# Feature pairs of a SwiGLU feed-forward in seven block products instead of eight, in a two-layer encoder step

## The chip, the cores and the metric

The kernel runs on one core of one Trainium2 chip, as one launch. The metric is device time in microseconds. TensorE (PE) multiplies, VectorE (DVE), ScalarE (ACT) and GpSimd (POOL) do everything else, and SyncE (SP) issues all DMAs.

## The reference

One inference step of a two-layer encoder on 512 prompt tokens and 8 x 16 sample tokens, T = 640 columns in all, D = 1024, F = 2816. It has four SwiGLU feed-forwards (two for each layer), a latent attention between the first two and a window attention between the last two:

```python
def swiglu(x, w_gate, w_up, w_down):
    return (jax.nn.silu(x @ w_gate) * (x @ w_up)) @ w_down
...
    for layer in range(DEPTH):
        x = x + FFN_RES * swiglu(rms_norm(x, P['ffn_norm1'][layer]), P['ffn1_w_gate'][layer],
                                 P['ffn1_w_up'][layer], P['ffn1_w_down'][layer])
        h = rms_norm(x, P['mix_norm'][layer])
...
        x = x + y
        x = x + FFN_RES * swiglu(rms_norm(x, P['ffn_norm2'][layer]), P['ffn2_w_gate'][layer],
                                 P['ffn2_w_up'][layer], P['ffn2_w_down'][layer])
```

## The kernel before

**Layout.** The residual stands transposed in SBUF: eight tiles of 128 of the 1024 model dimensions (`x`), each with 640 token columns, worked on in two halves h of 320 columns. A matrix product in fp32 is made of three products of split operands: every operand is a high part (fp32r, written by ScalarE as a copy) and a low part (the rest, a subtraction). `mm3` issues the three matmuls w_hi x_lo, w_lo x_hi, w_hi x_hi.

**A feed-forward** has 22 tiles of 128 features, taken as 11 pairs. For one feature tile the gate and the up tile take, for each half h, 2 x 8 blocks of the model dimension x 3 = 48 matmuls of 128x320 into `psa` (`pe_gate_up`). A pair is therefore 192 gate and up matmuls and 96 down matmuls: `pe_down` makes 16 outputs of 6 matmuls each into the four banks of `psb`. TensorE's order is: the gate and up products of pair p, then the down product of pair p-1. Before down output q it waits until VectorE has added output q-4 to the residual (`x_upd`).

**VectorE**, for every tile and half: two scalings of PSUM by the norm's factor (L667 gate, L668 up), after ScalarE's Silu (L606) the product (L674), after ScalarE's high part (L608) the low part (L676); then the 16 additions of the down outputs (L687).

**Weights.** A piece is eight 128x128 tiles (512 KB). A feature tile has three: gate, up, down. SyncE loads pieces in order into four slots of `raw` (L315); piece n waits until piece n-4 has been split, which is counted by `w_lo`. ScalarE writes the high part of a piece (L335), GpSimd the low part (L343), into `wa` (gate and up, two buffers) or `wb` (down, four buffers).

**Order.** All order is written out by hand: each engine has its own instruction list, and counting semaphores tie the lists together. Four of the five loop rounds of a feed-forward run over two pairs each as a hardware loop on ScalarE and GpSimd, the rest is unrolled.

Of the kernel before, what the change touches and what calls it, by code (L numbers as in the profile page):

```python
# [77 lines left out]
FIRST_PIECE = [sum(len(x) for x in PIECES[:u]) for u in range(len(UNITS) + 1)]  # L78
UNIT_OF = {name: [u for u, (n, _) in enumerate(UNITS) if n == name] for name, _ in UNITS}
# [37 lines left out]
GU = 2 * FT  # L117
# [41 lines left out]
def program(nc, a, ctx):  # L159
    sb = lambda name, cols, dt=F32: ctx.enter_context(nc.sbuf_tensor(name, [P, cols], dt))  # L160
    sem = lambda name: ctx.enter_context(nc.semaphore(name))

# [15 lines left out]
    acts = sb("acts", 2 * 4 * T, F32R)  # L178
    x = xs[:, :].rearrange("p (d t) -> p d t", t=T)
# [6 lines left out]
    ut = work[:, 4480:5120].rearrange("p (s t) -> p s t", t=HT)  # L186
    eps, eps_q = consts[:, EPS_COL:EPS_COL + 1], consts[:, EPS_COL + 1:EPS_COL + 2]
# [60 lines left out]
        "n_hi", "n_lo", "n_sq", "n_own", "n_sum", "n_std", "n_rstd", "n_gain"))  # L248
    warmed, warm_zero, warm_copy = sem("warmed"), sem("warm_zero"), sem("warm_copy")
# [43 lines left out]
    def used(u, j):  # L293

        name = UNITS[u][0]
        k = u - UNIT_OF[name][0]
        if name.startswith("ffn"):
            if j < 2:
                return gu_mm, GU * int(name[3]) + 2 * (k + 1)
            return out_mm, OUT_BASE[name] + N_OUT * (k // 2 + 1)  # L300
        if name == "wo":
            return out_mm, OUT_BASE[name] + OUT_USED[k]
        if name == "swao":
            return out_mm, OUT_BASE[name] + DT + (6, 3, 8)[k]
        return proj_mm, PROJ_BASE[name] + PROJ_USED[name][k]


    def load_piece(sp, u, j, it=None):

        p = FIRST_PIECE[u] + j  # L310
        if p >= RAW_SLOTS:
            sp.wait_ge(w_lo, at(it, 12, p - RAW_SLOTS + 1))
# [8 lines left out]
    def split_hi(act, u, j, it=None):  # L321

        p = FIRST_PIECE[u] + j
        act.wait_ge(landed[p % RAW_SLOTS], at(it, 48, 16 * (p // RAW_SLOTS + 1)))
        if SLOT_BEFORE[u, j]:
            s, v = used(*SLOT_BEFORE[u, j])
            if it is not None:

                name = UNITS[u][0] if UNITS[u][0].startswith("ffn") else UNITS[u - 1][0]
                k = u - UNIT_OF[name][0]  # L330
                s, v = (gu_mm, GU * int(name[3]) + 2 * (k - 1)) if j < 2 else (
                    out_mm, OUT_BASE[name] + N_OUT * ((k - 4) // 2 + 1))
            act.wait_ge(s, at(it, 8 if j < 2 else 32, v))
# [4 lines left out]
    def split_lo(pool, u, j, it=None):  # L338
        p = FIRST_PIECE[u] + j
        pool.wait_ge(w_hi, at(it, 12, p + 1))  # L340
# [3 lines left out]
                                hi[:, 0:n].bitcast(F32), ALU.subtract).then_inc(w_lo, 1)  # L344

# [8 lines left out]
    def mm3(ps, w, xx, first, last):  # L354

        nc.tensor.matmul(ps, w[0], xx[1], start=first, stop=False)  # L356
        nc.tensor.matmul(ps, w[1], xx[0], start=False, stop=False)  # L357
        return nc.tensor.matmul(ps, w[0], xx[0], start=False, stop=last)  # L358
# [69 lines left out]
    def act_start(act):  # L428
# [20 lines left out]
        split_hi(act, 2, 0)  # L449
        act_std(act, 0, 1)  # L450
        split_hi(act, 2, 1)
# [113 lines left out]

    def pe_down(pe, i, it, cc):
        u0 = UNIT_OF[f"ffn{i}"][0]
        base = OUT_BASE[f"ffn{i}"]
        pe.wait_ge(w_lo, at(it, 12, FIRST_PIECE[u0] + 6 * cc + 6))
        for q in range(N_OUT):  # L570
            d, h = ORDER[q]
            pe.wait_ge(x_upd, at(it, 32, base + 16 * cc + q - 3))
            if d == 0:
                pe.wait_ge(act_split, at(it, 8, GU * i + 4 * cc + 3 + h))
# [5 lines left out]
            if i == 3 and it is None and q == 11:  # L580
                pe.wait_ge(up_out, 4 * GU)
                pe_norm_sum(pe, N_FINAL, 0)

    def pe_ffn(pe, i, bank_free):
# [6 lines left out]
        with pe.Fori(0, FFN_LOOPS) as it:  # L591
            for cc in range(2):
                for off in (2 + 2 * cc, 3 + 2 * cc):
                    for h in range(2):
                        pe_gate_up(pe, i, it, off, h)
                pe_down(pe, i, it, cc)
        pe_down(pe, i, None, FT // 2 - 1)

    def act_gate_up(act, i, it, off):

        if i or off >= 2:
            act.wait_ge(out_mm, at(it, 32, OUT_BASE[f"ffn{i}"] + N_OUT * max(off // 2 - 1, 0)))
        for h in range(2):
            n = at(it, 8, GU * i + 2 * off + h + 1)
# [4 lines left out]

    def act_ffn(act, i):  # L610
        u0 = UNIT_OF[f"ffn{i}"][0]

        def tile_step(it, off):
            follows = u0 + off + 1 < len(UNITS)
            if i == 0 and it is None and off < 2:
                pass
            elif it is None and off == 0 and i != 2:
                act_std(act, N_FFN[i], 1)
            elif follows:
                split_hi(act, u0 + off + 1, 0, it)  # L620
                split_hi(act, u0 + off + 1, 1, it)
            early = it is None and off == 0 and i != 2
            if early and i:
                split_hi(act, u0 + 1, 2)
            act_gate_up(act, i, it, off)
            if follows and not early:
                split_hi(act, u0 + off + 1, 2, it)
        for off in range(2):
            tile_step(None, off)
        with act.Fori(0, FFN_LOOPS - 1) as it:  # L630
            for off in range(2, 6):
                tile_step(it, off)
        for off in range(FT - 4, FT):
            tile_step(None, off)

    def pool_ffn(pool, i):
        u0 = UNIT_OF[f"ffn{i}"][0]
        for off in range(2):
            for j in range(2 if i == 0 and off == 0 else 0, 3):
                split_lo(pool, u0 + off + 1, j)  # L640
        with pool.Fori(0, FFN_LOOPS - 1) as it:
            for off in range(2, 6):
                split_lo_unit(pool, u0 + off + 1, it)
        for off in range(FT - 4, FT):
            if u0 + off + 1 < len(UNITS):
                split_lo_unit(pool, u0 + off + 1)
# [7 lines left out]
    def sp_loop(sp, i):  # L654
        u0 = UNIT_OF[f"ffn{i}"][0]
        with sp.Fori(0, FFN_LOOPS) as it:
            for off in range(2, 6):
                load_unit(sp, u0 + off, it)

    def dve_scaled(dve, i, it, off, h):  # L660

        n = GU * i + 2 * off + h
        dve.wait_ge(gu_mm, at(it, 8, n + 1))
        if n >= 2:
            dve.wait_ge(act_split, at(it, 8, n - 1))
        banks = psb[:, 2 * h:2 * h + 2, 0:HT] if i == 0 and it is None and off == 1 else psa[:, 2 * h:2 * h + 2, 0:HT]
# [1598 lines left out]
```

## Time and profile before

| | us |
|---|---|
| median of three runs | 2534.16 |
| lowest and highest | 2527.32 and 2539.27 |
| the profiled execution, its own time | 2525.54 |
| its span, first to last instruction | 2523.7 |
| PE busy | 2455.3 (97%) |
| DVE busy | 1155.6 (46%) |
| ACT busy | 767.8 (30%) |
| POOL busy | 881.4 (35%) |

A span is cut into what each engine was busy with. A matmul's busy time is its latency, longer than the distance from one matmul to the next, so the cost of a matmul is read from the starts of neighbours. An engine's share of busy time is a mean over the whole program: whether a wait costs anything is read from the engine that waits for it.

### The profile page before, as it was taken

To read this page: it belongs to the slowest core of one execution; us is meant where nothing else is said; L and a number is where in the kernel's file an instruction comes from. 1 tells how busy PE (TensorE), PEld (TensorE's weight loads), DVE (VectorE), ACT (ScalarE), POOL (GpSimd) and SP (SyncE) were. 2 spreads that over 40 slices of the span, in tenths; PEclk is the share of its full clock that TensorE was granted. 3 is DMA by queue.
4 is the path that set the end of the run, shared out by engine and by line. 5 is a ranking of instruction groups with operands and counts; after the bars stand their busy time and mean duration, and the time that the engine had idled before them with its cause. 6 is when DMAs were issued, how large, how long until landed. Compare 5 with 4: busy or idle time off the path is not lost.

```text
span 2523.7 us, 42391 instructions
## 1 busy us (share of the span) xinstructions
PE 2455.3 (97%) x16448; PEld 2340.2 (93%) x16448; DVE 1155.6 (46%) x2378; ACT 767.8 (30%) x1505; POOL 881.4 (35%) x592
## 2 busy tenths in 40 slices
PE   8999999998999999999999999999999999999997
PEld 8999999987666999999999999999986899999997
DVE  6434343665355453434346434343455464343435
ACT  6121222423255332121215222222246432222223
POOL 2333333443123334242424433333245243333332
PEclk9999999999999999999999999999999999999998
DMA  5222223234242122222222321212123122222211
GB/s 171 76 75 75 75 75 91 94 137 158 80 149 82 59 76 83 67 79 70 77 73 76 93 91 58 91 58 90 52 105 104 40 93 76 75 75 75 75 50 42
DMA packets 72607, 210.80 MB, mean 84 GB/s; under 512 B 7681, under 2 KB 22049, under 8 KB 71745
## 3 DMA queue, kind: packets, MB, share of 16 engines
q1 hardware_dynamic: 72512, 209.55, 26.3%
q8 instruction: 58, 0.95, 0.2%
q14 instruction: 37, 0.30, 0.0%
HBM read 191.22 MB, written 18.30 MB: 83 GB/s over the span
## 4 chain that ended last, share of the span: by engine, by line
PE 88%; DVE 4%; issue 2%; ACT 2%; POOL 1%; SPq 1%; DMA 1%; DVEq 0%; ACTq 0%; POOLq 0%
PE psa L356 17%; PE psa L357 17%; PE psa L358 17%; PE psb L356 10%; PE psb L357 10%; PE psb L358 10%; DVE split L479 1%; PE psb L1032 1%; PE psa L1168 1%; PE psa L1001 1%; PE psb L1187 1%; DVE work L404 1%; PE psb L1175 1%; PE psa L1002 1%; POOL wa L343 1%
## 5 line engine op out<-in xcount | busy, mean ns | idle before, releaser
L356 PE MATMUL psa<-split,wa 128*128 128x320 f32 (+1 forms) x3040 | 944.5, 311 | 24.4 <-DVE split L479 16.8
L358 PE MATMUL psa<-split,wa 128*128 128x320 f32 x3024 | 935.8, 309 | 0.0
L357 PE MATMUL psa<-split,wa 128*128 128x320 f32 x3024 | 935.7, 309 | 0.0
L343 POOL TENSOR_TENSOR wb<-raw,wb 128x1024 fp32r<-128x1024 f32 (+1 forms) x99 | 235.4, 2378 | 1205.6 <-ACT wb L335 1178.4
L356 PEld LDWEIGHTS psa<-split,wa 128*128 128x128 f32 x3040 | 573.9, 189 | 28.5 <-DVE wa L461 9.6
L357 PEld LDWEIGHTS psa<-split,wa 128*128 128x128 f32 x3024 | 570.8, 189 | 0.9 <-issue 0.2
L358 PEld LDWEIGHTS psa<-split,wa 128*128 128x128 f32 x3024 | 570.5, 189 | 0.0
L343 POOL TENSOR_TENSOR wa<-raw,wa 128x1024 fp32r<-128x1024 f32 x205 | 490.4, 2412 | 169.8 <-ACT wa L335 169.8
L356 PE MATMUL psb<-acts,wb 128*128 128x320 f32 x1440 | 447.4, 311 | 1.9 <-DVE xs L687 1.7
L687 DVE SCALAR_TENSOR_TENSOR xs<-psb,xs 128x320 f32<-128x320 f32 x720 | 341.3, 488 | 229.6 <-PE psb L358 229.6
L357 PE MATMUL psb<-acts,wb 128*128 128x320 f32 x1440 | 444.7, 309 | 0.0
L358 PE MATMUL psb<-acts,wb 128*128 128x320 f32 x1440 | 444.6, 309 | 0.0
L667 DVE TENSOR_TENSOR work<-psa,work 128x320 f32<-128x320 f32 x174 | 85.4, 491 | 703.8 <-PE psa L358 703.7
L606 ACT ACTIVATE work<-work 128x320 f32<-128x320 f32 x176 | 83.0, 471 | 651.7 <-DVE work L667 651.7
L356 PEld LDWEIGHTS psb<-acts,wb 128*128 128x128 f32 x1440 | 270.6, 188 | 6.2 <-DVE xs L687 6.0
L357 PEld LDWEIGHTS psb<-acts,wb 128*128 128x128 f32 x1440 | 270.6, 188 | 0.2
L358 PEld LDWEIGHTS psb<-acts,wb 128*128 128x128 f32 x1440 | 270.6, 188 | 0.0
L335 ACT ACTIVATE wb<-raw 128x1024 fp32r<-128x1024 f32 (+1 forms) x101 | 104.9, 1039 | 467.7 <-PE psb L358 467.7
L335 ACT ACTIVATE wa<-raw 128x1024 fp32r<-128x1024 f32 x211 | 211.8, 1045 | 105.7 <-PE psb L358 43.9
L674 DVE TENSOR_TENSOR work<-work 128x320 f32<-128x320 f32 x176 | 174.2, 990 | 44.6 <-ACT work L606 44.6
L608 ACT ACTIVATE acts<-work 128x320 fp32r<-128x320 f32 x176 | 83.1, 472 | 200.9 <-DVE work L674 200.9
L676 DVE TENSOR_TENSOR acts<-work,acts 128x320 fp32r<-128x320 f32 x176 | 92.9, 528 | 94.6 <-ACT acts L608 94.6
(222 smaller groups left out, 2169.7 us busy)
## 6 DMA issues: line engine op xcount, KB each, us to landing
raw<-in_w SPq DMA_DIRECT2D x310, 512.0 KB, 3.9
park<-xs SPq DMA_DIRECT2D x2, 2560.0 KB, 9.0
work<-in_c_latT SPq DMA_DIRECT2D x8, 512.0 KB, 3.9
work<-in_c_lat SPq DMA_DIRECT2D x8, 512.0 KB, 3.6
xs<-park SPq DMA_DIRECT2D x1, 2560.0 KB, 14.5
xs<-park SPq DMA_DIRECT2D x2, 1280.0 KB, 5.5
y_out<-xs SPq DMA_DIRECT2D x8, 320.0 KB, 3.4
work<-v_park SPq DMA_DIRECT2D x8, 256.0 KB, 3.0
```

Source lines behind the costliest of these rows:

```text
L335: nc.scalar.activation(slots(u, j)[0][:, 0:n], raw[:, (p % RAW_SLOTS) * PIECE:(p % RAW_SLOTS) * PIECE + n], ACT.Copy).then_inc(w_hi, 1)
L343: nc.gpsimd.tensor_tensor(lo[:, 0:n], raw[:, (p % RAW_SLOTS) * PIECE:(p % RAW_SLOTS) * PIECE + n], hi[:, 0:n].bitcast(F32), ALU.subtract). ...
L356: nc.tensor.matmul(ps, w[0], xx[1], start=first, stop=False)
L357: nc.tensor.matmul(ps, w[1], xx[0], start=False, stop=False)
L358: return nc.tensor.matmul(ps, w[0], xx[0], start=False, stop=last)
L404: eng.tensor_tensor(acc[:, half(h)], acc[:, half(h)], sq[:, 3 * h + d % 3, :], ALU.add).then_inc(n_acc[h], 1)
L606: nc.scalar.activation(gt[:, h, :], gt[:, h, :], ACT.Silu).then_inc(silu_done, 1)
L608: nc.scalar.activation(act_hi[:, off % 4, half(h)], ut[:, h, :], ACT.Copy).then_inc(act_hid, 1)
L667: nc.vector.tensor_tensor(gt[:, h, :], banks[:, 0, :], rstd[:, half(h)], ALU.mult).then_inc(gate_out, 1)
L674: nc.vector.tensor_tensor(ut[:, h, :], gt[:, h, :], ut[:, h, :], ALU.mult).then_inc(prod_done, 1)
L676: nc.vector.tensor_tensor(act_lo[:, off % 4, half(h)], ut[:, h, :], act_hi[:, off % 4, half(h)].bitcast(F32), ALU.subtract).then_inc(act_s ...
L687: nc.vector.scalar_tensor_tensor(out=x[:, d, half(h)], in0=psb[:, q % 4, 0:HT], scalar=scale, in1=x[:, d, half(h)], op0=ALU.mult, op1=ALU. ...
```

## The change

From the second pair on, a pair of feature tiles (f), the two halves of the model dimension and the two halves of the columns (h) are a 2x2 by 2x2 block product. It is computed in seven block products (Strassen's scheme in Winograd's form) in place of eight, for gate and for up. The first pair stays as it was.

- TensorE: `pe_products` has 14 products (7 kinds, gate m=0 and up m=1) of 12 matmuls, 168 in place of 192. The kinds in order are a11, a12, s1, s2, s3, a22, s4. Down products are as before.
- Weight sides: three kinds are blocks of the weights as loaded, four are sums of half pieces, 512 columns wide. s3 and s1 are made on GpSimd (`sum_first`), s2 and s4 on VectorE (`sum_second`, `sum_fourth`), all but s3 in place in `raw`. Each of the 14 operands gets its high part from ScalarE and its low part from GpSimd in a ring of seven slots (`operand_hi`, `operand_lo`); the down pieces are split as before.
- Token sides: t1, t2, t3, n4 are made once in each feed-forward (`act_base`, `turn_first`, `turn_second`, `act_turn`, `turn_lo`) in `kvt`, `spare`, `work`.
- Results: partial sums in PSUM are copied by ScalarE at three points (`act_snap`, six copies a pair) and added by VectorE to other banks (`dve_mixed`, six a pair); the scaling by the norm is then a step of its own, with an SBUF source in six of eight (`dve_unmixed`).
- Pieces of a pair are loaded in the order gate f0, gate f1, up f0, up f1, down f0, down f1. A piece still waits for the release of the piece four places before it: the next pair's up f0 for the low part of this pair's down f0.
- Around the window attention, `kvt` is read back from `kv_out` and the loads of the sampled bias stand later in SyncE's list.

```diff
+KINDS = ("a11", "a12", "s1", "s2", "s3", "a22", "s4")
+TILE = [(0, 0), (1, 1), (1, 0), (0, 1)]
...
         p = FIRST_PIECE[u] + j
         if p >= RAW_SLOTS:
-            sp.wait_ge(w_lo, at(it, 12, p - RAW_SLOTS + 1))
+            place = ffn_place(p - RAW_SLOTS)
+            if place and place[2] < 4:
+                i, pair, n = place
+                sp.wait_ge(s_lo, at(it, 28, OPERANDS * i + OPS * (pair - 1) + 13 + n // 2))
+            else:
+                sp.wait_ge(w_lo, at(it, 4, N_SINGLE[p - RAW_SLOTS + 1]))
...
+    def sum_second(dve, i, it, pair, m):
+        dve.wait_ge(s_lo, at(it, 28, OPERANDS * i + OPS * (pair - 1) + m + 1))
+        dve.wait_ge(s_first, at(it, 8, SUMS * i + 4 * (pair - 1) + 2 * m + 2))
+        nc.vector.tensor_tensor(raw_half(i, pair, m, 0, 0), raw_half(i, pair, m, 1, 0), raw_half(i, pair, m, 0, 0), ALU.subtract).then_inc(s_sum, 1)
...
+    def pe_products(pe, i, it, pair):
+        for j in range(OPS):
+            pe.wait_ge(s_lo, at(it, 28, OPERANDS * i + OPS * (pair - 1) + j + 1))
+            if kind == "a11":
+                bank = psa[:, 2 * m, 0:HT]
+                pe.wait_ge(up_out, at(it, 8, PRODS * i + 4 * pair - 1 + m))
...
+    def act_pair(act, i, it, pair, follows=True):
+        act_snap(act, i, it, pair, 0)
+        o(6)
+        o(7)
+        act_snap(act, i, it, pair, 1)
+        o(8)
+        o(9)
+        o(10)
+        act_silu(act, i, it, pair, 0)
+        o(11)
+        act_prod(act, i, it, pair, 0)
+        o(12)
+        act_snap(act, i, it, pair, 2)
+        o(13)
+        act_snap(act, i, it, pair, 3)
+        act_snap(act, i, it, pair, 4)
+        act_snap(act, i, it, pair, 5)
+        act_silu(act, i, it, pair, 1)
+        split_hi(act, u0, 2, it)
+        act_prod(act, i, it, pair, 1)
+        act_silu(act, i, it, pair, 2)
+        split_hi(act, u0 + 1, 2, it)
+        after(0)
+        after(1)
+        act_prod(act, i, it, pair, 2)
+        act_silu(act, i, it, pair, 3)
+        after(2)
+        after(3)
+        act_prod(act, i, it, pair, 3)
+        after(4)
+        after(5)
...
+    def pool_pair(pool, i, it, pair, follows=True):
+        for j in range(6, OPS):
+            operand_lo(pool, i, it, pair, j)
+        split_lo(pool, u0, 2, it)
+        split_lo(pool, u0 + 1, 2, it)
+        if follows:
+            pool_operands(pool, i, it, pair + 1)
+    def pool_operands(pool, i, it, pair):
+        for m in range(2):
+            operand_lo(pool, i, it, pair, m)
+        for m in range(2):
+            sum_first(pool, i, it, pair, m, "s3")
+            sum_first(pool, i, it, pair, m, "s1")
+        for j in range(2, 6):
+            operand_lo(pool, i, it, pair, j)
...
+        turn_first(dve, i)
+        dve_scaled(dve, i, 1, 0)
+        dve_whole(dve, i, 1, 0)
+        turn_second(dve, i)
+        dve_scaled(dve, i, 1, 1)
+        dve_whole(dve, i, 1, 1)
+        for k in range(QUARTER):
+            turn_lo(dve, i, "t2", k)
+        for name in ("t3", "n4"):
+            for k in range(QUARTER):
+                turn_lo(dve, i, name, k)
+        def pair_step(it, pair, follows):
+            for m in range(2):
+                sum_second(dve, i, it, pair, m)
+            for m in range(2):
+                sum_fourth(dve, i, it, pair, m)
+            for c in range(3):
+                dve_tile(dve, i, it, pair, c)
+            dve_tile(dve, i, it, pair, 3)
+            for q, (d, h) in enumerate(ORDER):
+                dve_out(dve, base, it, N_OUT * (pair - 1), q, d, h, 0.5)
```

`act_pair` is ScalarE's whole list for a pair: `o(j)` is the high part of operand j of this pair, `after(j)` of the next pair. `up_out` counts the scaled up tiles, `s_lo` the operands' low parts.

ScalarE, in the loop of a feed-forward, before: a feature tile's two halves (Silu L606, high part L608) stand between splits of whole pieces (L335, `wa` gate and up, `wb` down).

```order
L335 ACTIVATE wa<-raw 128x1024 [waits gu_mm,w_landed1]
L335 ACTIVATE wa<-raw 128x1024 [waits gu_mm,w_landed2]
L606 ACTIVATE work<-work 128x320 [waits gate_out,out_mm]
L608 ACTIVATE acts<-work 128x320 [waits prod_done]
L606 ACTIVATE work<-work 128x320 [waits gate_out]
L608 ACTIVATE acts<-work 128x320 [waits prod_done]
L335 ACTIVATE wb<-raw 128x1024 [waits out_mm,w_landed3]
```

ScalarE at the same place after, from the Silu of the second result tile on: L800 is a Silu, L407 a down piece, L449 an operand's high part, L808 a product's high part.

```order
L800 ACTIVATE work<-work 128x320 [waits gate_out]
L407 ACTIVATE wb<-raw 128x1024 [waits out_mm,w_landed2]
L808 ACTIVATE acts<-work 128x320 [waits prod_done]
L799 REGISTER_ALU
L800 ACTIVATE work<-work 128x320 [waits gate_out]
L407 ACTIVATE wb<-raw 128x1024 [waits out_mm,w_landed3]
L435 REGISTER_ALU
L449 ACTIVATE wa<-raw 128x512 [waits gu_mm,w_landed0]
L449 ACTIVATE wa<-raw 128x512 [waits gu_mm,w_landed2]
L808 ACTIVATE acts<-work 128x320 [waits prod_done]
```

Between the third tile's Silu and its high part (the last row) there now stand a down piece and two operands of the next pair, the second of which waits for a piece in slot 2 of `raw`, the next pair's up f0.

VectorE at the end of a pair's tiles, before the first addition of the down product, before:

```order
L667 TENSOR_TENSOR work<-psa,work 128x320 [waits act_split,gu_mm]
L668 TENSOR_TENSOR work<-psa,work 128x320
L674 TENSOR_TENSOR work<-work 128x320 [waits silu_done,up_out]
L676 TENSOR_TENSOR acts<-work,acts 128x320 [waits act_hid]
L686 REGISTER_ALU
L687 SCALAR_TENSOR_TENSOR xs<-psb,xs 128x320 [waits out_mm]
```

VectorE at that place after: the third tile (scalings L954, product L960, low part L965), the fourth tile's sums L941 and scalings L954, the first down addition L1017, the fourth product L1067.

```order
L954 TENSOR_TENSOR work<-psa,work 128x320 [waits gu_mm] x2
L960 TENSOR_TENSOR work<-work 128x320 [waits silu_done,up_out]
L965 TENSOR_TENSOR acts<-work,acts 128x320 [waits act_hid]
L941 TENSOR_TENSOR work<-psa,work 128x320 [waits snapped,gu_mm] x2
L954 TENSOR_TENSOR work<-work 128x320 [waits mixed] x2
L1017 SCALAR_TENSOR_TENSOR xs<-psb,xs 128x320 [waits out_mm]
L1067 TENSOR_TENSOR work<-work 128x320 [waits silu_done,up_out]
```

The low part L965 stands ahead of four further instructions and of all down additions, and it waits for ScalarE's high part shown above.

## Rows read from the trace of the kernel before

**Rows 1.** The page: busy time of engines, and the chain that ended last.

```profile
PE 2455.3 (97%) x16448; PEld 2340.2 (93%) x16448; DVE 1155.6 (46%) x2378; ACT 767.8 (30%) x1505; POOL 881.4 (35%) x592
PE 88%; DVE 4%; issue 2%; ACT 2%; POOL 1%; SPq 1%; DMA 1%; DVEq 0%; ACTq 0%; POOLq 0%
```

**Rows 2.** Busy time in stretches of one pair: us, then each engine, PEclk, DMA.

```profile
102.20:144.40 42.20, 42.20 (x290) 42.20 (x289) 16.89 (x32) 9.53 (x14) 14.26 (x6) 1.00 0.25 75
144.40:186.60 42.20, 42.20 (x290) 42.20 (x289) 17.08 (x33) 9.57 (x14) 14.26 (x6) 1.00 0.25 75
```

**Rows 3.** Timeline of TensorE, two starts of `mm3`: start us, us, what.

```profile
300.09 0.31 PE L356 MATMUL psa<-split,wa 128*128 128x320 f32 x1
...
300.53 0.31 PE L356 MATMUL psa<-split,wa 128*128 128x320 f32 x1
```

**Rows 4.** Groups by form: xcount | busy us, mean ns | idle us before and releaser.

```profile
L343 POOL TENSOR_TENSOR wa<-raw,wa 128x1024 fp32r<-128x1024 f32 x205 | 490.4, 2412 | 169.8 <-ACT wa L335 169.8
L335 ACT ACTIVATE wa<-raw 128x1024 fp32r<-128x1024 f32 x211 | 211.8, 1045 | 105.7 <-PE psb L358 43.9 <-DMA raw<-in_w 37.0 <-PE psa L358 24.8
L608 ACT ACTIVATE acts<-work 128x320 fp32r<-128x320 f32 x176 | 83.1, 472 | 200.9 <-DVE work L674 200.9
```

**Rows 5.** Lines by themselves: durations ns min/median/max, first and last start.

```profile
L404 POOL TENSOR_TENSOR work<-work x63: 857/940/1249, 470.2 to 2499.2; 128x320 f32<-128x320 f32 x63
L461 DVE TENSOR_TENSOR wa<-raw,wa x4: 1219/1222/1225, 6.1 to 26.4; 128x1024 fp32r<-128x1024 f32 x4
L674 DVE TENSOR_TENSOR work<-work x176: 480/493/2555, 39.5 to 2477.2; 128x320 f32<-128x320 f32 x176
L667 DVE TENSOR_TENSOR work<-psa,work x174: 476/491/493, 35.7 to 2476.1; 128x320 f32<-128x320 f32 x174
L687 DVE SCALAR_TENSOR_TENSOR xs<-psb,xs x720: 474/490/493, 74.9 to 2508.0; 128x320 f32<-128x320 f32 x180
```

**Rows 6.** Timeline of VectorE in a pair; in brackets idle time before, and releaser.

```profile
319.18 0.48 DVE L668 TENSOR_TENSOR work<-psa,work 128x320 f32<-128x320 f32 x1
319.87 2.55 DVE L674 TENSOR_TENSOR work<-work 128x320 f32<-128x320 f32 x1 [0.21 <-ACT work L606]
322.96 0.49 DVE L676 TENSOR_TENSOR acts<-work,acts 128x320 fp32r<-128x320 f32 x1 [0.54 <-ACT acts L608]
...
328.35 1.68 DVE L687 SCALAR_TENSOR_TENSOR xs<-psb,xs 128x320 f32<-128x320 f32 x4
```

**Rows 7.** Timeline of GpSimd beside them.

```profile
317.31 4.76 POOL L343 TENSOR_TENSOR wa<-raw,wa 128x1024 fp32r<-128x1024 f32 x2
```

**Rows 8.** Timeline before the second feed-forward, VectorE and GpSimd both with SBUF sources.

```profile
867.14 1.16 DVE L491 TENSOR_TENSOR work<-xs 128x320 f32<-128x320 f32 x1
868.23 1.17 DVE L479 SCALAR_TENSOR_TENSOR split<-xs,consts,split 128x320 fp32r<-128x320 f32 x1
...
865.90 4.23 POOL L404 TENSOR_TENSOR work<-work 128x320 f32<-128x320 f32 x4 [1.23 <-ACT work L394]
```

**Rows 9.** The line of weight loads: time from issue to landing.

```profile
DMA to landing us min/median/max: 2.3/3.9/10.9
```

**Rows 10.** VectorE's timeline, first two tiles of the second feed-forward.

```profile
894.50 0.49 DVE L674 TENSOR_TENSOR work<-work 128x320 f32<-128x320 f32 x1
895.52 0.49 DVE L676 TENSOR_TENSOR acts<-work,acts 128x320 fp32r<-128x320 f32 x1 [0.54 <-ACT acts L608]
895.93 0.48 DVE L667 TENSOR_TENSOR work<-psa,work 128x320 f32<-128x320 f32 x1
...
902.44 0.49 DVE L667 TENSOR_TENSOR work<-psa,work 128x320 f32<-128x320 f32 x1 [0.57 <-PE psa L358]
```

**Rows 11.** Stretches around a stall of TensorE before the second feed-forward, as rows 2.

```profile
874.00:876.00 2.00, 0.31 (x1) 0.31 (x2) 2.00 (x3) 0.00 (x0) 1.28 (x1) 0.80 0.68 248
876.00:878.00 2.00, 2.00 (x8) 1.80 (x8) 2.00 (x6) 0.00 (x0) 0.00 (x0) 0.50 0.66 225
878.00:880.00 2.00, 2.00 (x12) 1.80 (x11) 2.00 (x6) 1.24 (x3) 0.00 (x0) 0.85 0.09 37
```

More of the change, by code:

```diff
@@ L78, with ffn_place, piece @@
 FIRST_PIECE = [sum(len(x) for x in PIECES[:u]) for u in range(len(UNITS) + 1)]
+FFN_AT = {name: FIRST_PIECE[u] for u, (name, _) in reversed(list(enumerate(UNITS))) if name.startswith("ffn")}
+PAIRS = FT // 2
+def ffn_place(p):
+    for name, first in FFN_AT.items():
+        if first + 6 <= p < first + 6 * PAIRS:
+            return int(name[3]), (p - first) // 6, (p - first) % 6
+    return None
+SINGLE = [int(ffn_place(p) is None or ffn_place(p)[2] >= 4) for p in range(FIRST_PIECE[-1])]
+N_SINGLE = [sum(SINGLE[:p]) for p in range(len(SINGLE) + 1)]
+def piece(u, j):
+    name = UNITS[u][0]
+    k = u - UNIT_OF[name][0]
+    if name.startswith("ffn") and k >= 2:
+        return FIRST_PIECE[u - k % 2] + 2 * j + k % 2
+    return FIRST_PIECE[u] + j
 UNIT_OF = {name: [u for u, (n, _) in enumerate(UNITS) if n == name] for name, _ in UNITS}
@@ L352, in split_lo_unit, with mm3 @@
             split_lo(pool, u, j, it)
[L354 to L358, printed above, removed]
+    def mm3(ps, w, xx, first, last, more=False):
+        nc.tensor.matmul(ps, w[0], xx[1], start=first, stop=False, skip_group_check=more)
+        nc.tensor.matmul(ps, w[1], xx[0], start=False, stop=False, skip_group_check=more)
+        return nc.tensor.matmul(ps, w[0], xx[0], start=False, stop=last, skip_group_check=more)
     def x_ready(eng, s, i):
@@ L628, in act_ffn @@
-        for off in range(2):
-            tile_step(None, off)
-        with act.Fori(0, FFN_LOOPS - 1) as it:
[L631 to L634, printed above, removed]
+        o = lambda j: operand_hi(act, i, None, 1, j)
+        if i != 2:
+            act_std(act, N_FFN[i], 1) if i else None
+            if i:
+                split_hi(act, u0 + 1, 2)
+        else:
+            split_hi(act, u0 + 1, 0)
+            split_hi(act, u0 + 1, 1)
@@ new lines, in dve_unmixed @@
+    def dve_unmixed(dve, i, it, pair, c):
+        h = TILE[c][1]
+        for m in range(2):
+            t = (gt, ut)[m][:, c % 2, :]
+            if c == 2:
+                dve.wait_ge(gu_mm, at(it, 28, GU * i + 4 + OPS * (pair - 1) + 11 + m))
+                source = psa[:, 2 * m, 0:HT]
+            else:
+                dve.wait_ge(mixed, at(it, 12, MIXES * i + 6 * (pair - 1) + 2 * (0, 1, None, 2)[c] + m + 1))
+                source = t
+            nc.vector.tensor_tensor(t, source, rstd[:, half(h)], ALU.mult).then_inc((gate_out, up_out)[m], 1)
```

390 lines of the change are left out of this document (293 added, 97 removed).

## Prediction

> **What bounds the kernel now.** The page's first two parts come first: TensorE is busy for 97% of the span and holds 88% of the chain that ended last [rows 1]. A feed-forward in its steady state has no hole at all: in a stretch of one pair TensorE is busy for all of 42.20 us at full clock, VectorE for 17, ScalarE for 9.5, GpSimd for 14.3 [rows 2]. `mm3` starts every 0.44 us [rows 3], 0.1467 us for a matmul; 192 + 96 = 288 matmuls give 42.2 us, which is that stretch. So matmuls taken away are paid back in full, as long as the other engines, now far from full, never make TensorE wait. The question is therefore not how busy they get, but which wait ends last.
>
> **What goes.** A pair has 24 matmuls fewer, and 40 pairs change (ten in each of four feed-forwards): 960 x 0.1467 = 140.8 us. In a pair, the 14 products of 1.76 us take 24.6 us instead of 28.2, the down product stays at 14.1, together 38.7 us instead of 42.2. This is the gain, and its ceiling.
>
> **What comes, as busy time.** A 512-wide step lies between a 320-wide and a 1024-wide one. On GpSimd that is between 0.86 and 2.41 us [rows 4, 5], 1.3 by a straight line; on ScalarE between 0.47 and 1.05 [rows 4], 0.6; on VectorE between 0.49 and 1.22 [rows 5], 0.7. GpSimd then has 14 low parts and 4 sums of 1.3 and two down pieces of 2.4: 28 us of 38.7. ScalarE has 14 x 0.6, 6 copies, 4 Silu and 4 high parts of 0.47, 2 pieces of 1.05: 17 us. VectorE has 16 additions, 14 sums and scalings, 8 tile steps of 0.4 to 0.5 and 4 weight sums of 0.7: 20 us. All fit, with GpSimd the nearest to its limit.
>
> **What VectorE meets.** A VectorE step with one source in PSUM never lasts longer than 0.493 us, whatever GpSimd does (L667, L687), while L674 with two sources in SBUF lasts up to 2.555 [rows 5]. The timeline shows why: at 319.87 it takes 2.55 us and ends just after GpSimd's instruction ends at 322.07 [rows 6, 7]. Where both have a queue of such steps they take turns: 1.16 us for each VectorE step beside GpSimd steps of 1.06 [rows 8]. Before, a pair has 8 such steps beside 14 us of GpSimd; after, it has 18 beside 28 us. Each can lose up to one GpSimd instruction, 1.3 us.
>
> **The step on which the forecast rests.** I walk one pair in its steady state; t is counted from its first product. The tenth product (s3, up) ends at 17.6. ScalarE's copy ends at 18.2, VectorE's sum at 18.7 and gate scaling at 19.1, Silu at 19.7. ScalarE's next entry is down f0, 1.05: 20.7. GpSimd's low part of it, 2.4: 23.1. Only now may SyncE load the next pair's up f0 into that slot: 3.9 us to landing [rows 9], 27.0. Its high part ends at 27.6. And behind it in ScalarE's list stands the high part of this pair's third tile: 28.1. VectorE waits for it (L965), and behind that wait stand the fourth tile's two sums and two scalings, and then the first addition of a down output. TensorE needs this addition for down output 4, at 24.6 + 4 x 0.88 = 28.2.
> If VectorE is never blocked: 28.5, 29.3, 30.1, addition done at 30.6: TensorE stands for 2.5 us. With the blocks that rows 6 to 8 show: the second down piece is done on GpSimd at 27.8 and the next pair's first low part runs until 29.1, so L965 ends at 29.5, the sums (PSUM source, free) at 30.3, the two scalings each wait for the end of a GpSimd instruction, 31.0 and 32.5, the addition at 32.9: 4.8 us, and the fourth product, blocked again, makes output 5 wait 0.7 more. Together 5.5 us. The bounds are 2.5 (no block) and 7.0 (a full block at each of the five two-source steps on this path); I take 5.5, since at that time GpSimd has eight instructions in a row to do and is never idle, as in rows 8. The last pair of a feed-forward has no next operands in ScalarE's list; there the wait hangs on the down pieces alone, and I take 2.0.
> Nothing else in the loop is late by the same walk: the copies before the accumulating products s3 and a22 are done 0.9 us or more ahead, weight operands are there by t = 40 for the next pair at 44, the down product's own operands are a pair old.
>
> **The start of each feed-forward.** In the second one VectorE is free at 895.9 and TensorE's fourth tile is done at about 902.4 [rows 10]. Now 12 token-side steps stand ahead of the scaling of the third tile and 8 more ahead of that of the fourth, and TensorE's second product waits for the latter. Unblocked that is 12 x 0.41 + 0.9 + 1.5 + 8 x 0.43 + 0.9 = 11.7 us, to 907.6, against 904.2 due; the 12 low parts and the first sum behind it make the seventh product late by some 7 us in all. With seven GpSimd instructions of 1.3 us in between it is 9 us more: 916, 12 us late. The bounds are 7 and 20 (the copy in front of s3 is then late as well, and the clock falls); I take 12, the value with the turns of rows 8. Four times: 48 us.
>
> **Edits at nothing.** The read-back of `kvt` and the bias loads start when the last gate and up product of the third feed-forward is done, with two down products (28 us) to cover them; uncovered they would be some 5 us. The token tables moved in `spare` and the new packing change no instruction.
>
> **The sum.** -140.8 + 36 x 5.5 + 4 x 2.0 + 4 x 12 = +113 us. The profiled execution took 2525.5 us (2.2 of it around the span); it is 8.6 below the median of the runs, 0.3%. On the median: 2534.2 + 113 = 2647 us. A steady pair should take 44.2 us.
>
> **Rivals.**
> (a) VectorE slips through between GpSimd's instructions: 40 x 2.5 + 4 x 7 - 140.8 = -13, 2521 us, and with half the blocks some 2560. For it: the median of L674 before is 0.493, so most steps met no block [rows 5]. Against it: GpSimd was idle for two thirds of the time then.
> (b) The other side, faster: the loop of loads closes early enough. It would need up f0 landed by t = 23, as when ScalarE reaches down f0 before the Silu or when the addition is not behind L965. Then only the starts cost: 2534 - 141 + 48 = 2441 us. It decides at an addition done by t = 28.2, 2.4 us earlier than the unblocked walk; the order rows speak against it, and all durations in that walk are measured ones.
> (c) Slower still: TensorE's clock. Behind a hole of 2.8 us the granted clock was 0.80, 0.50 and 0.85 in three stretches of 2 us, so the half level of 1.2 GHz for about 3 us [rows 11]: some 1.5 us lost. At each of 36 holes of 4.8 us that is 54 us more, 2701; with every block at its bound, 36 x 7 + 4 x 3 + 4 x 20 - 141 = +203, 2737.
> The Trainium skill (TensorE: Matmul & The Clock Gate, Part 1) has half clock as the state to which an idle array returns, and from which work lifts it again; taken at its word it makes (c) the rule and not the exception.
> I don't take it as the likeliest because the rows have such a hole only ahead of a feed-forward, in company of a second one, and none that stands alone between 39 us of full work.
> That the change does not do what it says is no rival: the built order has the 168 gate and up matmuls a pair.
>
> **How the numbers follow.** Forecast 0.50 (2590 to 2700), (a) 0.20 (2521 to 2590), (b) 0.14, (c) 0.16. A change within 0.5% (2521 to 2547) can't be told from none. Faster: (b) and a little of (a), 0.17. Same: 0.09 out of (a). Slower: 0.74. The range leaves out (b) and the far end of (c), together 0.19: 2510 to 2725.
>
> **What would show it.** Matmuls: 16448 - 960 = 15488. Right: a steady pair of about 44 us in which TensorE waits for the additions L1017 for 4 to 6 us in one place, VectorE's L965 waits for ScalarE's L808, and ScalarE's L449 waits for a load of `raw` once a pair; VectorE's L954 with SBUF sources has a mean near 1 us. Wrong: a pair of 39 us without holes (b); a wait for low parts of operands in the middle of the products, which would mean GpSimd itself is the bound; or a hole whose releaser is a copy of a partial sum.

## The result, and the profile after

The changed kernel takes 2718.88 us (median of 4 runs, 2709.79 to 2721.74), the kernel before 2531.82 us beside it (4 runs, 2527.32 to 2539.27). The ratio is 1.073, with an interval of 1.0692 to 1.0767: slower by 187 us, where +113 was forecast. The profiled execution has a span of 2715.3 us at a mean granted clock of 0.949, before 2523.7 us at 0.995.

Busy time of the engines and the chain that ended last, from the page of the changed kernel; these answer to [rows 1].

```profile
PE 2424.5 (89%) x15488; PEld 2287.3 (84%) x15488; DVE 1629.0 (60%) x2906; ACT 1048.9 (39%) x2225; POOL 1481.2 (55%) x1152
PE 28%; issue 27%; POOL 27%; DVE 10%; DMA 4%; ACT 3%; SPq 1%; POOLq 0%; DVEq 0%; ACTq 0%
```

960 matmuls are gone, but TensorE's busy time fell by 30.8 us and not by 140.8, and its idle time rose from 68.4 to 290.8 us. TensorE held 88% of the chain; now it holds 28%, and GpSimd, idle for 45% of the span, holds 27%. An engine that is busy for little more than half of the time can stand in this chain as long as TensorE does.

What TensorE waits for, from the list of waits (us in total, times, longest):

```profile
PE psb L492 <- DVE xs L1017: 167.5, 52, 5.8
PE psa L492 <- DVE work L933: 42.3, 8, 11.7
PE psa L492 <- DVE split L613: 17.8, 4, 9.8
PE psa L492 <- POOL wa L454: 11.6, 4, 3.2
```

The third was there before (16.8 us). The first is nearly all the hole in front of the down product's output 4: 40 of the 52 waits stand there, 36 of them 3.3 to 5.8 us long (4.3 on average), four, in the last pairs, 1.9. The second and fourth are the starts of the feed-forwards.

**One steady pair.** It starts at 291.8. Its whole stretch, and then six stretches of 2 us around the hole (columns as in [rows 2]):

```profile
291.80:336.80 45.00, 40.49 (x266) 40.22 (x265) 27.17 (x43) 15.91 (x30) 28.96 (x20) 0.96 0.21 70
318.00:320.00 2.00, 1.88 (x13) 1.62 (x12) 0.55 (x1) 0.99 (x2) 2.00 (x2) 1.00 0.00 0
320.00:322.00 2.00, 0.00 (x0) 0.00 (x0) 2.00 (x4) 0.00 (x0) 2.00 (x2) 1.00 0.72 195
322.00:324.00 2.00, 0.00 (x0) 0.00 (x0) 2.00 (x3) 1.50 (x3) 2.00 (x3) 1.00 0.17 68
324.00:326.00 2.00, 1.60 (x6) 1.60 (x7) 2.00 (x4) 0.56 (x3) 2.00 (x2) 0.58 0.00 0
326.00:328.00 2.00, 2.00 (x10) 2.00 (x9) 1.76 (x5) 0.44 (x1) 2.00 (x2) 0.56 0.00 0
328.00:330.00 2.00, 2.00 (x16) 2.00 (x15) 1.23 (x3) 0.63 (x1) 2.00 (x3) 1.00 0.00 0
```

A pair without a hole has 264 matmuls of 0.1467 us, 38.7 us; this one takes 45.0. There is one hole in it, and VectorE and GpSimd are both busy through all of it. Behind it the granted clock is 0.58 and 0.56 in two stretches, a mix of full clock and the half level of 1.2 GHz, and a count says the same: 6 and 10 matmuls in 2 us, then 16.

The queue behind it, in the timeline of ScalarE (start us, us, what; in brackets the idle time before):

```profile
315.89 1.04 ACT L407 ACTIVATE wb<-raw 128x1024 fp32r<-128x1024 f32 x1
316.84 0.61 ACT L449 ACTIVATE wa<-raw 128x512 fp32r<-128x512 f32 x1
318.42 0.63 ACT L449 ACTIVATE wa<-raw 128x512 fp32r<-128x512 f32 x1 [0.97 <-DMA raw<-in_w]
318.96 0.45 ACT L808 ACTIVATE acts<-work 128x320 fp32r<-128x320 f32 x1
```

of VectorE:

```profile
319.45 1.54 DVE L965 TENSOR_TENSOR acts<-work,acts 128x320 fp32r<-128x320 f32 x1 [2.87 <-ACT acts L808]
320.92 0.88 DVE L941 TENSOR_TENSOR work<-psa,work 128x320 f32<-128x320 f32 x2
321.71 2.23 DVE L954 TENSOR_TENSOR work<-work 128x320 f32<-128x320 f32 x2
323.86 0.48 DVE L1017 SCALAR_TENSOR_TENSOR xs<-psb,xs 128x320 f32<-128x320 f32 x1
```

of GpSimd:

```profile
312.33 2.40 POOL L415 TENSOR_TENSOR wb<-raw,wb 128x1024 fp32r<-128x1024 f32 x1 [5.59 <-ACT wb L407]
317.01 2.41 POOL L415 TENSOR_TENSOR wb<-raw,wb 128x1024 fp32r<-128x1024 f32 x1 [2.28 <-ACT wb L407]
319.37 2.75 POOL L454 TENSOR_TENSOR wa<-raw,wa 128x512 fp32r<-128x512 f32 x2
```

and of TensorE, the first product of output 4 and the next one:

```profile
324.40 0.63 PE L492 MATMUL psb<-acts,wb 128*128 128x320 f32 x1 [4.51 <-DVE xs L1017]
324.83 0.47 PE L493 MATMUL psb<-acts,wb 128*128 128x320 f32 x1
...
327.76 0.31 PE L492 MATMUL psb<-acts,wb 128*128 128x320 f32 x1
327.91 0.31 PE L493 MATMUL psb<-acts,wb 128*128 128x320 f32 x1
```

Read it from the end. TensorE waits 4.51 us for the first addition of a down output (L1017). That addition is a step of 0.48 us, and the product that it adds was done at about 317.3 (t = 25.5); it stands in VectorE's list behind L965, which waits for ScalarE's L808; that stands behind an L449, which waits for a weight load; that load waits for the slot which GpSimd's L415 at 312.33 frees. ScalarE's wait for the load occurs 36 times in the kernel, once in each steady pair that has a successor to load for:

```profile
ACT wa L449 <- DMA raw<-in_w: 35.6, 36, 1.4
```

Once VectorE is free, its two steps with PSUM sources (L941) take 0.44 us each, and its two with SBUF sources (L954) take 2.23 together, where two of them take 0.88 at 310.32, with GpSimd idle. Over the whole kernel (groups by form; xcount | busy us, mean ns | idle before):

```profile
L954 DVE TENSOR_TENSOR work<-work 128x320 f32<-128x320 f32 x240 | 210.0, 914 | 0.0
L965 DVE TENSOR_TENSOR acts<-work,acts 128x320 fp32r<-128x320 f32 x176 | 209.4, 1190 | 175.3 <-ACT acts L808 166.7 <-ACT acts L771 8.6
L954 DVE TENSOR_TENSOR work<-psa,work 128x320 f32<-128x320 f32 x80 | 35.0, 476 | 0.0
```

The same operation of the same line has a mean of 0.476 us with one source in PSUM and 0.914 with both in SBUF. The Trainium skill (SBUF — State Buffer, Who interferes with whom) says that a VectorE instruction with two SBUF inputs contends with a GpSimd instruction that reads SBUF, that contention for the port pair that they share is an exclusive lock, and that the order of issue decides which of the two blocks; these three lines agree with it.

### The profile page after: what moved, and what is told of

It reads as the page before. It is cut to its first block, busy times and chain, and to the rows that moved or that the text cites. A ratio compares the mean times of both kernels' runs of the same rounds, so it can differ in the third digit from the quotient of the medians.

```text
span 2715.3 us, 44983 instructions
## 1 busy us (share of the span) xinstructions
PE 2424.5 (89%) x15488; PEld 2287.3 (84%) x15488; DVE 1629.0 (60%) x2906; ACT 1048.9 (39%) x2225; POOL 1481.2 (55%) x1152
## 4 chain that ended last, share of the span: by engine, by line
PE 28%; issue 27%; POOL 27%; DVE 10%; DMA 4%; ACT 3%; SPq 1%; POOLq 0%; DVEq 0%; ACTq 0%
POOL wa L454 15%; POOL wb L415 6%; PE psb L492 4%; PE psb L493 4%; PE psb L494 4%; DMA raw<-in_w 3%; PE psa L492 3%; PE psa L494 3%; PE psa L493 3%; POOL wa_f L466 2%; POOL raw L468 2%; DVE split L613 1%; PE psb L1392 1%; PE psa L1528 1%; PE psa L1361 1%
## 5 line engine op out<-in xcount | busy, mean ns | idle before, releaser
L454 POOL TENSOR_TENSOR wa<-raw,wa 128x512 fp32r<-128x512 f32 x480 | 646.1, 1368 | 380.2 <-ACT wa L449 378.9
L492 PE MATMUL psb<-acts,wb 128*128 128x320 f32 x1440 | 484.6, 337 | 167.8 <-DVE xs L1017 167.5
L492 PE MATMUL psa<-split,wa 128*128 128x320 f32 (+1 forms) x1440 | 457.0, 317 | 67.5 <-DVE work L933 42.3
L1017 DVE SCALAR_TENSOR_TENSOR xs<-psb,xs 128x320 f32<-128x320 f32 x720 | 343.3, 486 | 233.0 <-PE psb L494 232.7
L493 PE MATMUL psb<-acts,wb 128*128 128x320 f32 x1440 | 472.9, 328 | 0.0
L494 PE MATMUL psb<-acts,wb 128*128 128x320 f32 x1440 | 471.8, 328 | 0.0
L415 POOL TENSOR_TENSOR wb<-raw,wb 128x1024 fp32r<-128x1024 f32 (+1 forms) x99 | 234.6, 2370 | 414.0 <-ACT wb L407 387.3
L492 PEld LDWEIGHTS psb<-acts,wb 128*128 128x128 f32 x1440 | 297.0, 206 | 187.2 <-DVE xs L1017 187.0
L493 PE MATMUL psa<-split,wa 128*128 128x320 f32 (+1 forms) x1424 | 446.5, 314 | 0.0
L494 PE MATMUL psa<-split,wa 128*128 128x320 f32 (+1 forms) x1424 | 446.2, 313 | 0.0
L449 ACT ACTIVATE wa<-raw 128x512 fp32r<-128x512 f32 x480 | 290.0, 622 | 164.0 <-POOL raw L468 73.1
L492 PEld LDWEIGHTS psa<-split,wa 128*128 128x128 f32 x1440 | 277.4, 193 | 74.0 <-DVE work L933 44.8
L965 DVE TENSOR_TENSOR acts<-work,acts 128x320 fp32r<-128x320 f32 x176 | 209.4, 1190 | 175.3 <-ACT acts L808 166.7
L795 ACT ACTIVATE work<-psa 128x320 f32<-128x320 f32 x240 | 104.7, 436 | 501.7 <-PE psa L494 500.9
L493 PEld LDWEIGHTS psb<-acts,wb 128*128 128x128 f32 x1440 | 297.2, 206 | 0.2
L494 PEld LDWEIGHTS psb<-acts,wb 128*128 128x128 f32 x1440 | 295.7, 205 | 0.0
L493 PEld LDWEIGHTS psa<-split,wa 128*128 128x128 f32 x1424 | 274.0, 192 | 0.8
L494 PEld LDWEIGHTS psa<-split,wa 128*128 128x128 f32 x1424 | 273.9, 192 | 0.0
L954 DVE TENSOR_TENSOR work<-work 128x320 f32<-128x320 f32 x240 | 210.0, 914 | 0.0
L415 POOL TENSOR_TENSOR wa<-raw,wa 128x1024 fp32r<-128x1024 f32 x45 | 109.0, 2440 | 173.2 <-ACT wa L407 173.2
L493 PE MATMUL psa<-spare_r,wa 128*128 128x320 f32 x640 | 199.6, 312 | 0.0
L494 PE MATMUL psa<-spare_r,wa 128*128 128x320 f32 x640 | 199.6, 312 | 0.0
```

Source lines behind the costliest of these rows:

```text
L415: nc.gpsimd.tensor_tensor(lo[:, 0:n], raw[:, (p % RAW_SLOTS) * PIECE:(p % RAW_SLOTS) * PIECE + n], hi[:, 0:n].bitcast(F32), ALU.subtract). ...
L449: nc.scalar.activation(ring_hi[:, (j + RING_AT[i]) % RING, :], operand(i, pair, kind, m), ACT.Copy).then_inc(s_hi, 1)
L454: nc.gpsimd.tensor_tensor(ring_lo[:, r, :], operand(i, pair, KINDS[j // 2], j % 2), ring_hi[:, r, :].bitcast(F32), ALU.subtract).then_inc( ...
L492: nc.tensor.matmul(ps, w[0], xx[1], start=first, stop=False, skip_group_check=more)
L493: nc.tensor.matmul(ps, w[1], xx[0], start=False, stop=False, skip_group_check=more)
L795: nc.scalar.activation(snap[:, n, :], psa[:, 2 * m, 0:HT], ACT.Copy).then_inc(snapped, 1)
```

## The experiments

Each was timed beside the kernel before, and the ratios are to that. Two theories stood at the start. **The queue:** the load chain delays L965, and the additions stand behind it. **GpSimd:** its 28 us of work per pair, and its blocking of VectorE, make the pair long wherever the additions stand.

**The third tile's high part earlier in ScalarE's list.** It no longer stands behind the high part of the next pair's up f0, which waits for the load.

```
+        act_prod(act, i, it, pair, 2)
         split_hi(act, u0 + 1, 2, it)
         after(0)
         after(1)
-        act_prod(act, i, it, pair, 2)
```

> ScalarE's list alone is changed: the high part of a pair's third tile stands ahead of the second down piece and of the next pair's first two operands. If the wait for the load of the next pair's up f0 is what delays the additions, L965's counterpart no longer waits for it: its end moves from t = 29.2 to about 25.7, but the two scalings behind it now meet GpSimd's low part of the second down piece, so that the first addition is done at about 31.1 instead of 32.5. Hole 3.0 us instead of 4.4, and less half clock: 1.4 to 2.5 us in each of 36 pairs, 2630 to 2670 us. If GpSimd's port alone makes the hole, wherever the high part stands: 2700 us or more.

2658.51 us, ratio 1.0501 (1.0479 to 1.0523), 60 us under the changed kernel, in the range expected. TensorE's wait for the additions, and VectorE's two scalings behind L965 in a steady pair:

```profile
PE psb L492 <- DVE xs L1017: 128.0, 72, 4.7
357.51 4.00 DVE L954 TENSOR_TENSOR work<-work 128x320 f32<-128x320 f32 x2
```

ScalarE's wait for the load is gone (0.4 us in one place, where the changed kernel has 35.6), and VectorE's L965 waits 81.7 us for L808 instead of 166.7. The wait for the load is a cause, but not the last: with it gone, the two scalings meet GpSimd's low part of the second down piece (L415, 357.30 to 359.68) and take 4.00 us, so the first addition still ends late.

**The additions first in VectorE's list.** Four additions come ahead of the third tile's low part, and the rest of the third and fourth tile is spread among the later ones. The operations are the same.

```
+            dve_unmixed(dve, i, it, pair, 2)
+            dve_times(dve, i, it, pair, 2)
             for q, (d, h) in enumerate(ORDER):
                 dve_out(dve, base, it, N_OUT * (pair - 1), q, d, h, 0.5)
+                if q == 3:
+                    dve_prod_lo(dve, i, it, pair, 2, 0, (2 * pair + 1) % 4, 0)
+                    dve_mixed(dve, i, it, pair, 3)
+                if q == 4:
+                    dve_unmixed(dve, i, it, pair, 3, (0,))
+                if q == 5:
+                    dve_unmixed(dve, i, it, pair, 3, (1,))
+                if q == 7:
+                    dve_times(dve, i, it, pair, 3)
+                if q == 9:
+                    dve_prod_lo(dve, i, it, pair, 3, 1, (2 * pair) % 4, 1)
```

> VectorE's list alone is changed: the first four additions of the down product stand ahead of the third tile's low part, and the rest of the third and fourth tile is spread between the later additions. If the hole comes from additions queued behind the wait for the load, it goes away: a steady pair of about 39 us, and 2480 to 2520 us in all, since only the starts of the feed-forwards cost more than before. If GpSimd's or VectorE's own load is the bound, TensorE waits in another place and a pair stays above 42 us: 2600 us or more.

2468.55 us (2461.36 to 2469.04), ratio 0.9737 (0.9714 to 0.9759): 250 us under the changed kernel and 2.6% under the kernel before. It came out 11 us below the range expected. A stretch of a steady pair, and TensorE's waits; that for the additions is all but gone:

```profile
262.60:301.10 38.50, 38.50 (x265) 38.50 (x264) 29.09 (x43) 15.71 (x30) 31.21 (x21) 1.00 0.24 82
```
```profile
PE psa L492 <- DVE work L933: 42.2, 8, 11.8
PE psa L492 <- POOL wa L454: 11.8, 4, 3.2
PE psb L492 <- DVE xs L1023: 4.6, 11, 0.8
ACT wa L449 <- DMA raw<-in_w: 35.6, 36, 1.3
```

TensorE is busy in all of 38.50 us at full clock, with GpSimd busy for 31.2 of it; from pair to pair it is 38.72 us, where the kernel before has 42.24. The theory that GpSimd's load bounds the pair falls. ScalarE still waits for the load 36 times, 35.6 us in all, as in the changed kernel: that wait costs nothing where no addition stands behind it. And VectorE is blocked more than in the changed kernel, not less: its busy time is 1715.3 us for the same steps instead of 1629.0, with its weight sums slower by more than that and other steps a little faster:

```profile
L474 DVE TENSOR_TENSOR raw<-raw 128x512 f32<-128x512 f32 x80 | 122.0, 1563 | 1.4 <-issue 0.2
```

That is 1.563 us a step where the changed kernel has 0.684, and it costs TensorE nothing. A blocked step matters only where it stands ahead of something that is due.

**Both edits.** The two edits above together.

> Both edits together. If the queue behind L965 is the whole cause, the early high part adds nothing to the additions put first: within 10 us of that kernel. If each edit takes away a part of its own, it is faster than either by 20 us or more.

2473.04 us, ratio 0.977 (0.9748 to 0.9793), 4.5 us above the additions first alone. With the additions out of the queue, the early high part gives nothing more.

**TensorE kept busy in the hole.** The start of down output 4 is preceded by 24 matmuls whose result nobody reads (960 in all, 141 us at 0.1467).

```
+            if q == 4 and it is not None:
+                pe.wait_ge(up_out, at(it, 8, PRODS * i + 4 * cc + 7))
+                for _ in range(24):
+                    nc.tensor.matmul(psa[:, 0, 0:HT], sp_hi[:, 0, 0:P], sp_hi[:, 0, 0:HT], start=True, stop=True)
             pe.wait_ge(x_upd, at(it, 32, base + 16 * cc + q - 3))
```

> In the hole ahead of down output 4, TensorE does 24 matmuls of 128x320 (3.5 us) whose result nobody reads; everything else is as in the changed kernel. If the half clock behind each hole costs time of its own, the granted clock stays at 1.0 there and a pair gets 0.8 to 1.5 us shorter: 2655 to 2690 us, in spite of 3.5 us of additional work a pair. If the clock costs nothing because the additions set the pace anyway: 2719 us or a little more.

2682.47 us, ratio 1.0587 (1.0567 to 1.0607): 36 us **less** with 141 us of matmuls more. The same pair's stretch, three of the 2 us stretches, and the wait that is left:

```profile
291.80:336.80 45.00, 43.59 (x295) 43.06 (x294) 27.45 (x44) 16.80 (x33) 29.05 (x20) 1.00 0.20 70
...
322.00:324.00 2.00, 1.14 (x6) 0.88 (x6) 2.00 (x5) 0.53 (x2) 2.00 (x2) 1.00 0.00 0
324.00:326.00 2.00, 1.90 (x13) 1.90 (x14) 2.00 (x6) 0.67 (x2) 2.00 (x2) 1.00 0.00 0
326.00:328.00 2.00, 2.00 (x15) 2.00 (x15) 1.29 (x4) 0.63 (x1) 2.00 (x3) 1.00 0.00 0
```
```profile
PE psb L492 <- DVE xs L1021: 52.4, 71, 2.9
```

The clock stays at 1.00 behind the hole. TensorE's busy time is 2510.9 us; without the 141 us of these matmuls 2370, against 2424.5 in the changed kernel. So 54 us of its busy time there was the half clock, of which 36 come back as time; filler and waits together, 193 us, are longer than the 167.5 us of waits that they replace. The starts of the down matmuls say the same: in the 36 steady pairs of the changed kernel the matmuls behind the hole that start more than 0.2 us apart cost 69 us over 0.1467 each, here 11.

**One source of the fourth tile's scalings in PSUM.** They read the bank of the last product, not the sum in SBUF, so this kernel leaves the partial sum of that tile out, and two more steps a pair have a PSUM source.

```
-                source = t
+                source = psa[:, 2 * m + 1, 0:HT] if c == 3 else t
```

> The changed kernel, but the two scalings of the fourth tile read TensorE's bank in PSUM in place of the sum in SBUF, so that they have one source in SBUF and not two; the partial sum is left out of that tile, its output is another. If GpSimd's instructions hold such two-source steps up, the two scalings last 0.4 us each and not 2.2 together, the hole gets 1.3 to 1.4 us shorter: 2650 to 2680 us. If the wait for the load alone sets the hole and the scalings' length is hidden: 2710 us or more.

2642.91 us, ratio 1.0433 (1.041 to 1.0457), 76 us less, 7 us below the range expected. VectorE's timeline between L965 and the first addition, in a steady pair:

```profile
310.09 1.58 DVE L965 TENSOR_TENSOR acts<-work,acts 128x320 fp32r<-128x320 f32 x1 [2.83 <-ACT acts L808]
311.59 0.87 DVE L941 TENSOR_TENSOR work<-psa,work 128x320 f32<-128x320 f32 x2
312.39 0.87 DVE L954 TENSOR_TENSOR work<-psa,work 128x320 f32<-128x320 f32 x2
313.19 0.47 DVE L1017 SCALAR_TENSOR_TENSOR xs<-psb,xs 128x320 f32<-128x320 f32 x1
```

The two scalings take 0.87 us here and 2.23 in the changed kernel; all else in the row of steps is as long as there. That is 1.36 us a pair, 49 us in 36 pairs. The gain per pair is 2.1 us. By the starts of the down matmuls in the 36 steady pairs, 1.5 us of it are shorter waits (4.6 us a pair down to 3.15, where the second wait, for output 5, is gone) and 0.5 are fewer matmuls at half clock (1.9 us a pair down to 1.4).

**The down piece earlier.** ScalarE splits the pair's first down piece ahead of the second tile's Silu, so the load chain starts earlier.

```
+        split_hi(act, u0, 2, it)
         act_silu(act, i, it, pair, 1)
-        split_hi(act, u0, 2, it)
```

> The changed kernel, but ScalarE's high part of the first down piece stands ahead of the second tile's Silu: the load chain that ends in the next pair's up f0 starts 1.4 us earlier, with nothing else moved on VectorE. If this chain sets the end of L965, the hole gets up to 1.4 us shorter, less where GpSimd's instruction boundary decides: 2650 to 2700 us. If it does not: 2719 us within 8.

2673.96 us (5 runs, 2669.88 to 2687.71), ratio 1.0543 (1.0519 to 1.0566): 45 us less, in the range expected. TensorE's wait, in the profiled execution, which at 2687.71 us was the longest of the five:

```profile
PE psb L492 <- DVE xs L1017: 135.4, 66, 5.9
```

ScalarE's wait for the load is down to 1.6 us, in five places. An edit at the head of the load chain shortens TensorE's hole at its other end; the early high part did it by taking L808 out from behind the load. The two together show the load chain as what L965 waits for.

**The start of a feed-forward in another order.** On top of the additions first, the scalings of the third and fourth tile stand ahead of the low parts of `t1` and the sums of `t3` and `n4`.

```
         turn_first(dve, i)
         dve_scaled(dve, i, 1, 0)
         dve_whole(dve, i, 1, 0)
-        turn_second(dve, i)
+        for k in range(QUARTER):
+            turn_lo(dve, i, "t1", k)
         dve_scaled(dve, i, 1, 1)
         dve_whole(dve, i, 1, 1)
+        turn_second(dve, i)
```

> On top of the kernel with the additions first (2468 us): at the start of a feed-forward the scalings of the third and fourth tile stand ahead of the token-side low parts of t1 and of the sums t3 and n4. If the order of VectorE's list at the start is what TensorE's 42 us of waits for L933 are, they shrink to under 25 us and the time falls by 15 to 35 us: 2433 to 2453 us. If the token-side work as such is the bound, TensorE waits as long for the operands or the low parts behind it: within 5 us of 2468.

2463.15 us (2459.29 to 2470.41), ratio 0.9715 (0.9692 to 0.9739): this can't be told from the additions first alone, and the theory fell that the order of VectorE's list is what the start costs. The waits say where it went:

```profile
PE psa L492 <- DVE work L933: 26.7, 8, 5.9
PE psa L492 <- POOL wa L454: 23.2, 4, 6.8
```

L933's wait fell by 15.5 us and the wait for GpSimd's low parts rose by 11.4. In the second feed-forward of this run four of VectorE's token-side steps (L995) still take 5.05 us beside four steps of GpSimd. As I read it, the two take turns at work that the first products all need, so another order moves the wait and doesn't shorten it; that reading has no experiment of its own.

**All of it.** Additions first, the other start and the early down piece.

> Additions first, the start's order and the first down piece early, together. Once the additions are on time the load chain has slack, so the early piece adds nothing: within 6 us of the kernel with additions first and the start's order, 2430 to 2455 us.

2471.49 us, ratio 0.9748 (0.9725 to 0.9771), 8 us above the start's order. The early down piece gives 45 us where the additions wait for L965, and nothing where they don't. Both numbers expected were missed: the range was built on a gain at the start that is not there, and 8 us are more than the 6 allowed.

## Why the prediction was right, and where it was not

**The sign, the place and the mechanism held.** The walk gave t = 27.0 for the landing of up f0, 29.5 for the end of L965, 31.0 and 32.5 for the scalings and 32.9 for the first addition. Measured in the pair above (t = 0 at 291.8), they are 26.6, 29.2, 32.1 for both scalings and 32.5. A walk through three in-order lists, with durations from the kernel before, found the end of the hole to 0.4 us; no busy share shows a hole at all. The additions first confirm it by removing it: 250 us. One part of the walk did not hold: output 5 was to wait 0.7 us more, and it waits in 8 of the 36 pairs only, 0.2 to 0.35 us.

**Rival (c) won over the forecast.** 2719 us lies above the 2590 to 2700 of the likeliest case and in (c)'s 2701 to 2737; the whole range, 2510 to 2725, reached from a small gain to a large loss and held it by 6 us only. The terms, forecast and measured:

| Term | forecast us | measured us | from |
|---|---|---|---|
| matmuls removed | -141 | -141 | 960 fewer at 0.1467 |
| steady pairs | +198 | +232 | from the first down matmul of the first changed pair to that of the tenth (90.88 to 497.10 in the first feed-forward) it is 407.5 us on average, 349.5 with the additions first; four times the difference |
| last pairs | +8 | +9 | their down products take 2.2 us more each than with the additions first |
| elsewhere | 0 | +9 | what is left of the 250 us between these two kernels; in the traces 7 of it lie between the first and the second feed-forward, and were not followed up |
| starts | +48 | +78 | 2468.5 less (2531.5 - 140.8) |
| sum | +113 | +187 | |

Two terms were mis-sized, and what was missing in both is mostly the clock. **The holes:** I put 5.5 us on a pair, all of it waits. In the pair above TensorE waits 4.5, then 12 matmuls start 0.267 us apart instead of 0.147, 1.4 us more, and the first of them adds some 0.3: together 6.3. Over the 36 steady pairs, counted from the starts of the down matmuls, it is 6.55 us: 4.6 for the waits, less than forecast, and 1.9 for 11 to 23 matmuls at the slower distance. The step that failed is the one on the clock, a term that I left out: that a hole standing alone between 39 us of full work would not bring the half level. It does, in all 36. (c) had put 54 us on it; by the starts it is 69, and the filler takes 54 us out of the busy time. That (c)'s 2701 comes within 18 us of the time is luck in part: its waits were too long by 0.9 us a pair, 32 us, its starts and its half clock too short by 30 and 15. The rule of the Trainium skill (TensorE: Matmul & The Clock Gate, Part 1), an idle array falls back to half clock and work must lift it again, was the better guide than the lack of such a hole in the rows. **The starts:** the waits for L933 and for GpSimd's low parts are 54 us together (13.5 for each start, where 12 was forecast). Most of the other 24 is of the kind of this stretch, in the second feed-forward:

```profile
960.00:965.00 5.00, 0.00 (x0) 0.00 (x0) 5.00 (x5) 0.00 (x0) 5.00 (x4) 0.76 0.00 0
965.00:970.00 5.00, 3.23 (x12) 3.17 (x12) 4.19 (x9) 0.94 (x2) 0.57 (x1) 0.50 0.00 0
```

a wait of 7.3 us and then the clock at 0.50. Counted between the down products of one feed-forward and the next, and ahead of the first, matmuls that start 0.2 to 0.5 us apart cost 20 us more with the additions first than in the kernel before; no experiment took them away. What fills the wait is the blocking of [rows 8], four steps each in 5.04 and 5.95 us from the moment when GpSimd starts its own, at 955.00, where four steps of the same shape had just taken 1.94:

```profile
953.14 1.94 DVE L985 SCALAR_TENSOR_TENSOR kvt<-xs,consts,acts_f 128x320 f32<-128x320 f32 x4
955.00 5.04 DVE L989 SCALAR_TENSOR_TENSOR spare<-xs,consts,kvt 128x320 f32<-128x320 f32 x4
959.97 5.95 DVE L1012 TENSOR_TENSOR kvt_r<-kvt,kvt_r 128x320 fp32r<-128x320 f32 x4
```

**Rival (a)** fell: VectorE did not slip through. The two scalings are blocked, and experiment and trace put 1.4 to 2.1 us a pair on it. **Rival (b)** is what the additions first give, 2468 us where 2441 was worked out for a loop without holes; the difference of 27 us is the 30 us by which the starts were too short. **The estimates of busy time** held: the 512-wide steps measured 1.30 us at the median on GpSimd (1.37 at the mean) for 1.3, 0.62 on ScalarE for 0.6 and 0.68 on VectorE for 0.7; only GpSimd's four sums took 1.5 each, 0.8 us more a pair, for which there was cover. **The edits at nothing** left no wait of their own among those of TensorE.

## What to carry to other kernels

Removing work from the engine that bounds a kernel pays only as far as it then doesn't wait for another engine: walk one iteration through every in-order list it touches, and look for short, due steps behind long waits. Here the same instructions in another order are worth 250 us of 2719, and turn a loss of 7.3% into a gain of 2.6%. Count each hole of the matrix engine at more than its length (here 4.3 us of waiting on average cost 6.5), and put the steps with two SBUF sources where nothing is due behind them if GpSimd works beside them.

## What the runs showed of the hardware that I had not expected

- A hole of 4.5 us, between 39 us of unbroken matmuls, put the granted clock at 0.58 and 0.56 in the two stretches of 2 us behind it, and 11 to 23 matmuls behind each of the 36 such holes (3.3 to 5.8 us) started later than 0.2 us after one another, mostly 0.267, instead of 0.147; unread matmuls in the hole kept it at 1.00 and made the kernel 36 us faster although 960 matmuls were added.
- Blocking between VectorE and GpSimd depends on when their queues meet, not on the counts: L474 has a mean of 0.684 us in the changed kernel and 1.563 with the additions first, the operation, the shape and the number of GpSimd's steps (1152) being equal.
- GpSimd's sums of two parts of `raw` (128x512) take 1.525 and 1.493 us on average, and the first of them never less than 1.506 in the changed kernel, while its subtractions of a high part, of the same shape, have a median of 1.296. With the additions first, the same sums come down to 1.287 at the least, so the shape alone doesn't make the difference; what does was not tested.
